# A two-block network in one program: a last weighted sum on TensorE, skipped expert blocks with other waits, keys rounded by two engines, one early load

## The chip, the cores and the metric

The kernel runs on one core of one Trainium2 chip. The core has five engines that run in parallel, each with its own list of instructions, and they meet only through semaphores: TensorE (PE in the rows; PEld is its weight load), VectorE (DVE), ScalarE (ACT), GpSimd (POOL), and SyncE (SP), which here does nothing but start DMAs. The metric is the device time of one execution in microseconds. A change is faster, the same or slower by the times of both kernels in turn on one chip.

## The reference

The computation is two transformer-like blocks over 2048 tokens of width 1024, all in 32-bit floats, then a last norm.

```python
def first_block(x, ...):
        h = _rms_norm(x, pre_norm_g[l]);  z = h @ w_in[l]
        z_q, z_kv, z_kr, g_attn, u_ssm, g_ssm = jnp.split(z, split_points, axis=-1)
        attn = _mla_attention(z_q, z_kv, z_kr, positions, ...)      # 4 heads, one shared rotary key
        ssm = _s5_bidirectional(u_ssm, ...)                         # 32 groups of 64 states
        mixed = jnp.concatenate([attn, ssm], axis=-1) @ w_out[l]
        x = x + _rms_norm(mixed, post_norm_g[l])

def second_block(x, c, ctx, ...):
        attn_x = _attend(qa, [ka_c, ka], [va_c, va])                # 8 heads over 2 key heads, 2304 keys
        ret_x = _ret_output(_retention_latent(...), ...)
        x_new = x + gt1 * (jnp.concatenate([attn_x, ret_x], axis=-1) @ w_out[l])
        y = _hier_moe(h2, ...)                                      # 2 of 32 experts for each token
        x_new = x_new + gt2 * y
    return _rmsnorm(x, final_norm_g)
```

In the mixture of experts, each token goes to two experts. Tokens are sorted by expert and padded to blocks of 128, so that one block has one expert: `(silu(x @ w_gate) * (x @ w_up)) @ w_down`. The result of a token is the sum of its two rows, each times its weight. How many blocks are needed depends on the data: at most 63.

## The kernel before

The program is a row of stages. Each is a block of code with one function for each engine, and a stage starts when every engine has left the one before. Tokens are worked in 16 tiles of 128. Between stages the data lies in DRAM (`between_...` tensors). In the order of time: `project_1`, `attention` (first block), `s5`, `mix_1`, `project_2`, `attention_2`, `retention`, `mix_2`, `dispatch`, `experts`, `combine`.

Many products are made exact enough out of TensorE's faster float format (F32R in the code): a matrix is split into a high part, which fits that format, and a low part, the rest; then three products (high by high, high by low, low by high) are added up. Each split costs a rounding and a subtraction on other engines.

**attention** (`attention`, from L730). The keys are split once, before and within the first tile: five sets of 128 by 2048 (one rotary set and four heads). For each set, VectorE masks the low bits (`high_part`, L723), writes the high part (L1066) and subtracts 5/8 of the columns (L1067), and GpSimd subtracts 3/8 (L864). The raw keys are loaded into two buffers `KX`, so set n waits for the split of set n - 2. Head 0 needs two sets, each later head one; VectorE does the set of head h + 1 right behind the scale of head h (`top_of`, L1028). TensorE's scores of a head (L916) wait for both subtractions. In the tiles behind the first, no key is split.

**mix_1** (from L1408). The states `YS` are loaded in two halves of the columns (L1454), the first by SP and ACT. Its tile loop writes x1 to DRAM. In turn 4 SP loads the first bank of the next stage's weights.

**project_2** (from L1749). X of tile 0 is loaded (L1818), squared, scaled, turned by TensorE, modulated and split (L1922 to L1991); then ACT and DVE split five banks of weights in turn (L1972, L2055), each as it arrives, and TensorE starts a bank when its split is done (L1898).

**attention_2** (from L2060). 32 units (16 tiles by 2 key heads) of 18 steps. A step is a score, exp (L2246) and rounding (L2248) on ACT, a subtraction on GpSimd (L2145), and three products. Ahead of a unit, TensorE and VectorE find the maximum of all scores (L2168, L2278). At the start VectorE splits queries and keys, and behind unit 0's maxima the keys of head 1 and both heads of values (L2256, L2258, L2306).

**experts** (from L3073). For each block, SP loads the three weight matrices (2 MB each) if the expert is new, GpSimd gathers 128 rows of tokens by index (L3165) into one of two buffers, ACT and DVE split the weights, and TensorE multiplies. `tiles_in_use` runs a fixed loop over pairs of blocks on each engine; for pairs that no token needs it calls `skipped`, in which each engine only waits for and increments the semaphores that a real block would. TensorE's `skipped` waits for the gathered rows of the next block (L3238), and GpSimd gathers for the skipped blocks too. Behind the loop, one block's hidden values are turned (L3184), multiplied down (L3197), moved (L3270) and stored (L3126).

**combine** (from L3374). For each of 16 tiles, with buffers for 8:

```python
Y1 = w1 * Y1            # ACT, L3434: first gathered row by its weight
Y1 = w2 * Y2 + Y1       # DVE, L3453
Y1 = Y1 * gate          # DVE, L3455
X2 = Y1 + X2            # DVE, L3458
rstd from sum(X2^2)     # ACT, L3427, L3429, then DVE, L3444
Y1 = X2 * rstd * final_g  # DVE, L3446, one tile behind
```

GpSimd gathers Y2 and Y1 of a tile by index (L3416, L3420); SP loads X2, the constants `gate` (L3399) and `final_g` (L3400), and stores the result (L3395). VectorE starts once both constants are there (L3448). The gather of Y1 of tile i + 8 waits until the store of tile i has landed.

## Time and profile before

| what | value |
|---|---|
| median of three runs | 4704.63 us (4699.98 to 4708.75) |
| profiled execution, its own time | 4703.52 us |
| its span, first to last instruction | 4701.7 us |
| TensorE busy | 4155.1 us (88%), mean granted clock 0.944 |
| VectorE busy | 3094.2 us (66%) |
| ScalarE busy | 2335.9 us (50%) |
| GpSimd busy | 1238.6 us (26%) |
| moved by DMA | 701.06 MB |

Busy shares are means over eleven stages with different limits, so they don't say what one stage is worth. The rows further down are read stage by stage: where an instruction starts, what its engine waited for, and how long the group takes. In a row of a timeline, the bracket at the end is the idle time of the engine just ahead of the instruction and what ended it. Granted clock 1.00 is 2.4 GHz of TensorE, 0.50 is 1.2 GHz.

### The profile page before, as it was taken

How to read it: one execution, taken by the hardware profiler on the slowest of the kernel's cores; microseconds unless marked ns; L12 is line 12 of the kernel's file. 1: busy time of each engine (PE TensorE's matmuls, PEld its weight loads, DVE VectorE, ACT ScalarE, POOL GpSimd, SP SyncE). 2: the span in 40 equal slices, each digit the busy share in tenths (PEclk: the TensorE clock that was granted, in tenths of full speed). 3: DMA queues.
4: the chain of work that ended last, by engine and by line, in shares of the span. 5: the costliest groups of instructions: out<-in, count | busy, mean ns of one | idle time of the engine just before them, and what ended most of it. 6: DMA issues, size and time to landing. Idle time of an engine off the chain costs nothing. (4 is left out here: it accounts for less than half of the span.)

```text
span 4701.7 us, 62499 instructions
## 1 busy us (share of the span) xinstructions
PE 4155.1 (88%) x21994; PEld 3447.7 (73%) x21994; DVE 3094.2 (66%) x3968; ACT 2335.9 (50%) x3681; POOL 1238.6 (26%) x805
## 2 busy tenths in 40 slices
PE   7999879999886997999799999997698699999960
PEld 5777668998765886888678788785476588888850
DVE  6676555555476775444477776766655799999866
ACT  3434323333311554323288888883322477777743
POOL 0000032222110000000189999990000022222222
PEclk9999989999998998999899999998899799999985
DMA  5344331111277333222330000008533488888957
GB/s 181 132 150 136 132 116 56 55 55 55 90 219 207 130 100 125 70 67 72 97 138 14 21 14 14 17 9 280 193 129 117 192 335 317 342 328 342 399 217 299
DMA packets 357224, 701.06 MB, mean 149 GB/s; under 512 B 62928, under 2 KB 244304, under 8 KB 339152
## 3 DMA queue, kind: packets, MB, share of 16 engines
q1 hardware_dynamic: 327984, 618.04, 37.8%
q0 software_dynamic: 13824, 50.34, 2.8%
q10 hardware_dynamic: 15264, 30.81, 2.0%
q8 instruction: 78, 1.28, 0.1%
q14 instruction: 74, 0.61, 0.0%
HBM read 585.06 MB, written 194.51 MB: 166 GB/s over the span
## 5 line engine op out<-in xcount | busy, mean ns | idle before, releaser
L2145 POOL TENSOR_TENSOR a_PL<-a_PT,a_PH 128x512 fp32r<-128x512 f32 x576 | 764.9, 1350 | 81.0 <-ACT a_PH L2248 79.9
L3165 POOL DMA_INDIRECT e_XG<-between_h,all_slots x64 | 214.1, 3346 | 1179.9 <-PE e_pT L3173 642.8
L2278 DVE TENSOR_REDUCE a_part<-a_pA 128x1 f32<-128x1024 f32 (+1 forms) x384 | 366.9, 958 | 238.3 <-PE a_pA L2168 235.2
L2246 ACT ACTIVATE a_PT<-a_pB 128x512 f32<-128x512 f32 x576 | 341.1, 592 | 104.3 <-PE a_pB L2191 102.9
L2248 ACT ACTIVATE a_PH<-a_PT 128x512 fp32r<-128x512 f32 x576 | 364.2, 632 | 18.4
L1021 DVE TENSOR_REDUCE a_maxima<-a_pS 128x1 f32<-128x512 f32 x256 | 176.8, 691 | 169.1 <-PE a_pS L916 168.2
L857 POOL TENSOR_TENSOR a_QL<-a_RQ,a_QT 128x512 fp32r<-128x512 f32 x16 | 20.6, 1290 | 987.7 <-DVE a_QP L1056 958.2
L994 ACT ACTIVATE a_PT<-a_pT 128x512 f32<-128x512 f32 x128 | 69.5, 594 | 415.8 <-PE a_pT L934 415.8
L948 PE MATMUL a_pO<-a_V,a_PT 128*128 128x128 f32 x2048 | 249.4, 275 | 0.3 <-DVE a_PT L1034 0.3
L948 PEld LDWEIGHTS a_pO<-a_V,a_PT 128*128 128x128 f32 x2048 | 243.4, 192 | 5.9 <-DVE a_PT L1034 0.6
L2168 PE MATMUL a_pA<-a_KH,a_QA 128*128 128x512 f32 (+1 forms) x640 | 201.3, 382 | 44.3 <-DVE a_KH L2256 17.7
L2203 PE MATMUL a_pO<-a_PH,a_VH 128*128 128x512 f32 x576 | 228.0, 396 | 0.0
L2190 PE MATMUL a_pB<-a_QA,a_KH 128*128 128x512 f32 x576 | 226.1, 392 | 0.7 <-ACT a_QA L2234 0.7
L2206 PE MATMUL a_pO<-a_PL,a_VH 128*128 128x512 f32 x576 | 225.2, 391 | 1.1 <-POOL a_PL L2145 1.1
L2191 PE MATMUL a_pB<-a_QA,a_KL 128*128 128x512 f32 x576 | 225.6, 392 | 0.0
L2204 PE MATMUL a_pO<-a_PH,a_VL 128*128 128x512 f32 x576 | 225.5, 391 | 0.0
L2134 POOL MEMSET a_QA<- 64x1024 f32 x2 | 1.8, 944 | 846.4 <-POOLq L1751 846.4
L3324 DVE TENSOR_TENSOR e_gate_low<-w_gate,e_gate_high 128x4096 fp32r<-128x4096 f32 x48 | 212.2, 4420 | 10.0 <-ACT e_gate_high L3256 9.7
L3256 ACT ACTIVATE e_gate_high<-w_gate 128x4096 fp32r<-128x4096 f32 x48 | 174.4, 3632 | 82.5 <-SPq L3129 45.6
L3256 ACT ACTIVATE e_up_high<-w_up 128x4096 fp32r<-128x4096 f32 x47 | 170.8, 3635 | 86.2 <-DMA w_up<-in_moe_w_up 78.5
L3324 DVE TENSOR_TENSOR e_up_low<-w_up,e_up_high 128x4096 fp32r<-128x4096 f32 x47 | 207.5, 4415 | 2.3 <-ACT e_up_high L3256 2.3
L3324 DVE TENSOR_TENSOR e_down_low<-w_down,e_down_high 128x4096 fp32r<-128x4096 f32 x47 | 207.6, 4417 | 0.0
(552 smaller groups left out, 10707.7 us busy)
## 6 DMA issues: line engine op xcount, KB each, us to landing
w_gate<-in_moe_w_gate SPq DMA_DIRECT2D x49, 2048.0 KB, 7.6
w_up<-in_moe_w_up SPq DMA_DIRECT2D x48, 2048.0 KB, 11.8
w_down<-in_moe_w_down SPq DMA_DIRECT2D x47, 2048.0 KB
between_yb<-e_Y SPq DMA_DIRECT2D x47, 512.0 KB, 7.3
between_x<-m_X SPq DMA_DIRECT2D x32, 512.0 KB, 3.0
r_W<-in_w_ada SPq DMA_DIRECT2D x8, 2048.0 KB, 21.0
between_yb<-a_zeros SPq DMA_DIRECT2D x31, 512.0 KB, 12.9
between_tv<-p_OV SPq DMA_DIRECT2D x16, 576.0 KB, 2.8
```

The source lines that it names most:

```text
L948: mm = pe.matmul(pO[:, 0:dv], PT[:, jj, :], values(V, h, jj), start=jj == 0, stop=jj == key_tiles - 1)
L2145: pool.tensor_tensor(PL[:, t % RING, :], PT[:, t % RING, :], PH[:, t % RING, :].bitcast(F32), ALU.subtract).then_inc(S["p_low"], 1)
L2190: pe.matmul(pB[t % 2][:], KH[g][:, tile], QA1[i % 2][:, heads, :], start=True, stop=False)
L2191: pe.matmul(pB[t % 2][:], KL[g][:, tile], QA2[i % 2][:, heads, :], start=False, stop=True).then_inc(S["s_ps"], 1)
L2203: pe.matmul(pO[u % 2][:], VH[:, j, g, :], high, start=first, stop=False)
L2204: pe.matmul(pO[u % 2][:], VL[:, j, g, :], high, start=False, stop=False)
L2206: pe.matmul(pO[u % 2][:], VH[:, j, g, :], low, start=False, stop=last).then_inc(S["o_ps"], 1)
L2246: act.activation(PT[:, t % RING, :], pB[t % 2][:], ACT.Exp, scale=scale).then_inc(S["p_ready"], 1)
L2248: act.activation(PH[:, t % RING, :], PT[:, t % RING, :], ACT.Copy).then_inc(S["p_high"], 1)
L2278: dve.tensor_reduce(part[:, h, r % (NG2 // G4):r % (NG2 // G4) + 1], src, AX_X, ALU.max).then_inc(S["maxed"], 1)
L3256: act.activation(WH[n][:], raw(n, t)[:], ACT.Copy).then_inc(w_high[n], 1)
L3324: dve.tensor_tensor(WL[n][:], raw(n, t)[:], WH[n][:].bitcast(F32), ALU.subtract).then_inc(w_low[n], 1)
```

## The change

It has seven parts.

1. **attention**: keys are loaded straight into `KL`, all five sets without a wait. The high part is made by one instruction (the write in F32R rounds): by VectorE for set 0, by ACT for the others. The subtraction works in place. GpSimd takes 3/8 of every set but set 1, which VectorE does whole.
2. **mix_1**: the first part of the states is a quarter of the columns, the second three quarters.
3. **x_first**: SP loads tile 0 of x1 in turn 6 of `mix_1` into a buffer that `project_2` uses as its first.
4. **project_2**: the first bank of weights is split ahead of the modulation (ACT) and of the low part (DVE) of tile 0.
5. **attention_2**: ACT rounds the keys and one part of the first queries, GpSimd subtracts for the keys, and the values of head 1 are split one unit later.
6. **experts**: in `skipped` each engine waits only for its own earlier work; GpSimd waits itself for its gather before last. Behind its loop, SP loads all of x2 (four DMAs of 2 MB) into the buffers of the weights. ACT issues the last store.
7. **combine**: ACT makes two diagonal matrices of the weights of each tile, and TensorE adds up the two gathered tiles with four matmuls of 128 by 512 in plain F32 in PSUM; VectorE reads that sum with the gate. The x2 tiles are read where they were loaded.

```diff
 # attention
-                    if n >= 2:
-                        sp.wait_ge(S["k_split"], n - 1)
-                        sp.wait_ge(S["k_split_dve"], n - 1)
                     for rows, src in key_sets[n]:
-                        sp.dma_start(KX[n % 2][rows, :], src).then_inc(k_loaded[n], 16)
+                        sp.dma_start(KL[n][rows, :].bitcast(F32), src).then_inc(k_loaded[n], 16)
...
+        def lower(eng, n, keys):
+            raw = KL[n][:, keys].bitcast(F32)
+            return eng.tensor_tensor(KL[n][:, keys], raw, KH[n][:, keys].bitcast(F32), ALU.subtract)
...
+                    if n != 1:
+                        high_known(pool, n)
+                        lower(pool, n, pool_keys).then_inc(S["k_split"], 1)
...
                     exps(t, h, h % 2)
-
+                    if t.first and h + 3 < len(key_sets):
+                        high_keys(h + 3)
+            def high_keys(n):
+                act.wait_ge(k_loaded[n], 16 * len(key_sets[n]))
+                act.activation(KH[n][:], KL[n][:].bitcast(F32), ACT.Copy).then_inc(S["k_high_act"], 1)
+            high_keys(1)
+            high_keys(2)
...
+                    if n == 0:
+                        dve.wait_ge(k_loaded[0], 16 * len(key_sets[0]))
+                        dve.tensor_copy(KH[0][:], KL[0][:].bitcast(F32)).then_inc(S["k_high"], 1)
+                    high_known(dve, n)
+                    lower(dve, n, slice(0, nk) if n == 1 else dve_keys).then_inc(S["k_split_dve"], 1)
 # mix_1
-            cols = slice(half * NCH // 2, (half + 1) * NCH // 2)
+            cols = (slice(0, NCH // 4), slice(NCH // 4, NCH))[half]
...
+                if i == 6:
+                    sp.wait_ge(stored[0], 32)
+                    sp.dma_start(M["x_first"][:], D["x1"][0:P, :]).then_inc(M["x_first_loaded"], 16)
 # project_2, ACT (the same order on DVE with weights_low and low)
+            square_sum(tile_at(0))
+            for n in range(EARLY):
+                weights_high(n)
+            modulate(tile_at(0))
+            for n in range(EARLY, len(BANKS2)):
+                weights_high(n)
 # attention_2
+            for g in range(HKV):
+                pool.wait_ge(S["k_high"], g + 1)
+                pool.tensor_tensor(KL[g][HD:P, :], KX[g][HD:P, :], KH[g][HD:P, :].bitcast(F32), ALU.subtract).then_inc(S["k_split"], 1)
...
+            act.wait_ge(q_loaded[0], 32)
+            act.activation(QA2[0][HD:P], RQ[0][HD:P], ACT.Copy).then_inc(S["q_high_act"], 1)
+            for g in range(HKV):
+                act.wait_ge(k_loaded[g], 32)
+                act.activation(KH[g][:], KX[g][:], ACT.Copy).then_inc(S["k_high"], 1)
...
+            high_values(0)
             row(0)
+            high_values(1)
...
             split_queries(0)
-            split_keys(0)
             for r in range(NG2):
                 maximum(0, r)
             top_of(0)
-            split_keys(1)
-            for g in range(HKV):
-                dve.wait_ge(S["v_high"], g + 1)
-                dve.tensor_tensor(VL[:, :, g, :], ...)
+            low_values(0)
...
+                if u == 0:
+                    low_values(1)
 # experts: SP behind its loop
+            sp.wait_ge(w_low["gate"], NB + 1)
+            sp.wait_ge(w_low["up"], NB)
+            sp.wait_ge(w_low["down"], NB)
+            rows = D["x2"].rearrange("(n p) d -> p n d", p=P)
+            for n, space in enumerate(M["X2"]):
+                sp.dma_start(space[:].rearrange("p (n d) -> p n d", d=DM), rows[:, 4 * n:4 * n + 4, :]).then_inc(M["x2_loaded"][n], 16)
...
                 if i >= 2:
                     pool.wait_ge(S["t_ps"], i - 1)
+                    pool.wait_ge(x_loaded[i % 2], 16 * (i // 2))
...
+            for b in range(2):
+                pool.wait_ge(x_loaded[b], 16 * (NB // 2 + 1))
 # experts: TensorE's skipped (ACT, DVE and SP in the same way)
-                pe.wait_ge(S["xt_low"], i + 1)
-                pe.wait_ge(w_low["gate"], i + 1)
-                pe.wait_ge(S["silu_ready"], i)
-                pe.wait_ge(S["hh_ready"], i)
+                pe.wait_ge(S["u_ps"], i)
+                pe.wait_ge(S["d_ps"], i)
+                pe.wait_ge(S["t_ps"], i + 1)
+                pe.wait_ge(S["g_ps"], i)
                 pe.sem_inc(S["ht_ps"], 1)
                 pe.sem_inc(S["g_ps"], 1)
-                pe.wait_ge(x_loaded[nxt.b], 16 * nxt.n + 16)
                 pe.sem_inc(S["t_ps"], 1)
...
+            pe.wait_ge(S["ht_high"], NB - 1)
+            pe.wait_ge(S["ht_low"], NB - 1)
             hidden_transposed(tile_at(NB - 1))
 # combine
+            for i in range(NT):
+                for n in range(2):
+                    d = act.activation(diagonal[n][:, i, :], C["ident"][:], ACT.Copy, scale=M["weights"][:, n, i:i + 1])
+                d.then_inc(S["diagonal_ready"], 1)
...
+                pe.wait_ge(y1_loaded[b], 16 * (i // DEEP + 1))
+                for h in range(2):
+                    cols = slice(h * BANK, (h + 1) * BANK)
+                    pe.matmul(pS[i % len(pS)][:, h, :], diagonal[0][:, i, :], Y1[b][:, cols], start=True, stop=False)
+                pe.wait_ge(y2_loaded[b], 16 * (i // DEEP + 1))
+                for h in range(2):
+                    cols = slice(h * BANK, (h + 1) * BANK)
+                    mm = pe.matmul(pS[i % len(pS)][:, h, :], diagonal[1][:, i, :], Y2[b][:, cols], start=False, stop=True)
+                mm.then_inc(S["sum_ready"], 1)
...
-                dve.scalar_tensor_tensor(Y1[b][:], Y2[b][:], M["weights"][:, 1, i:i + 1], Y1[b][:], ALU.mult, ALU.add).then_inc(S["sum_ready"], 1)
                 dve.wait_ge(S["sum_ready"], i + 1)
-                dve.tensor_tensor(Y1[b][:], Y1[b][:], gate[:], ALU.mult).then_inc(S["gated"], 1)
+                dve.tensor_tensor(Y1[b][:], pS[i % len(pS)][:].rearrange("p a b -> p (a b)"), gate[:], ALU.mult).then_inc(S["gated"], 1)
```

## Rows read from the trace of the kernel before

**Rows 1.** Chain that ended last, last stage: start us, us, what
```profile
4675.99 1.29 DVE c_Y L3453
...
4691.74 1.28 DVE c_Y L3446
```
**Rows 2.** Timeline from the last experts to the last stage: start us, us, engine, line
```profile
4577.43 0.94 POOL L3165 DMA_INDIRECT e_XG<-between_h,all_slots  x1 [1.48 <-PEq L3238]
4583.25 1.11 PE L3184 MATMUL e_pH<-all_ident,e_HH 128*128 128x128 f32 x4 [42.82 <-DVEq L3366]
4594.50 0.36 SPq L3126 DMA_DIRECT2D between_yb<-e_Y  x1
4598.17 0.94 POOL L3416 DMA_INDIRECT c_Y<-between_yb,all_dest  x1 [19.80 <-PEq L3376]
4609.75 1.28 DVE L3453 SCALAR_TENSOR_TENSOR c_Y<-c_Y,all_weights 128x1024 f32<-128x1024 f32 x1 [24.04 <-ACT c_Y L3434]
```
**Rows 3.** Busy time in a stretch: PE, PEld, DVE, ACT, POOL, PEclk, DMA share, GB/s
```profile
4624.00:4676.00 52.00, 0.00 (x0) 0.00 (x0) 50.96 (x52) 26.87 (x43) 16.14 (x15) 0.50 1.03 419
```
**Rows 4.** DMA of 4604 to 4620: queue, packets, MB, share; then the last stage's issue
```profile
q0 software_dynamic: 912, 3.34, 51.3%
...
c_final_g<-in_final_g SPq DMA_DIRECT2D x1, 512.0 KB, 8.6
```
**Rows 5.** DMA issues of 4540 to 4598: queue, times, median us to landing
```profile
e_XG<-between_h,all_slots POOLq DMA_INDIRECT x14, 5.0
```
**Rows 6.** VectorE's last semaphore line in skipped blocks: ns min/median/max, first and last start
```profile
L3366 DVEq EVENT_SEMAPHORE  x16: 21/21/21, 4545.9 to 4583.1; - x16
```
**Rows 7.** Timeline of the retention stage: 32 matmuls in plain F32
```profile
3215.44 14.00 PE L2622 MATMUL r_pR<-r_W,r_alone 128*128 128x512 f32 x32 [0.88 <-DMA r_W<-in_w_ada]
```
**Rows 8.** Waits of 578 to 700, the start of the first attention
```profile
PE a_pS L916 <- POOL a_KL L864: 36.5, 4, 23.6
```
**Rows 9.** Timeline of the same start: first key mask, first scores, scales of heads 0, 3, 4
```profile
589.10 1.23 DVE L723 TENSOR_SCALAR a_KT<-a_KX 128x2048 int32<-128x2048 int32 x1 [3.01 <-DMA a_KX<-between_kr]
...
600.38 0.76 PE L916 MATMUL a_pS<-a_KH,a_QP 128*128 128x512 f32 x1 [23.61 <-POOL a_KL L864]
...
607.66 0.15 DVE L1028 TENSOR_SCALAR a_bias<-a_top 128x1 f32<-128x1 f32 x1
...
653.75 0.15 DVE L1028 TENSOR_SCALAR a_bias<-a_top 128x1 f32<-128x1 f32 x1
...
663.70 0.15 DVE L1028 TENSOR_SCALAR a_bias<-a_top 128x1 f32<-128x1 f32 x1
```
**Rows 10.** Its key instructions: ns min/median/max, first and last start
```profile
L1067 DVE TENSOR_TENSOR a_KL<-a_KX,a_KT x5: 1481/1484/1484, 591.5 to 641.3; 128x1280 fp32r<-128x1280 f32 x5
...
L864 POOL TENSOR_TENSOR a_KL<-a_KX,a_KT x5: 2910/2982/2983, 591.7 to 641.5; 128x768 fp32r<-128x768 f32 x5
```
**Rows 11.** Timeline of the start of the second projection
```profile
1818.66 1.06 ACT L1922 ACTIVATE p_HF<-p_X 128x1024 f32<-128x1024 f32 x1 [9.40 <-DMA p_X<-between_x]
...
1826.23 3.60 ACT L1972 ACTIVATE p_WH<-p2w_w_in 128x4096 fp32r<-128x4096 f32 x1
...
1834.43 3.75 PE L1898 MATMUL p_pZ<-p_WH,p_HH 128*128 128x512 f32 x8 [11.29 <-DVE p2w_w_in L2055]
...
1841.67 3.64 ACT L1972 ACTIVATE p_WH<-p_WL 128x4096 fp32r<-128x4096 f32 x1 [1.78 <-DMA p_WL<-between_w_in]
...
1850.55 2.00 PE L1898 MATMUL p_pZ<-p_WH,p_HH 128*128 128x512 f32 x8
```
**Rows 12.** Timeline of the start of the second attention
```profile
2357.30 7.99 POOL L2145 TENSOR_TENSOR a_PL<-a_PT,a_PH 128x512 fp32r<-128x512 f32 x3 [18.90 <-ACT a_PH L2248]
...
2362.87 2.67 DVE L2278 TENSOR_REDUCE a_part<-a_pA 128x1 f32<-128x1024 f32 x3
...
2366.94 1.28 POOL L2145 TENSOR_TENSOR a_PL<-a_PT,a_PH 128x512 fp32r<-128x512 f32 x1 [1.65 <-ACT a_PH L2248]
```
**Rows 13.** Timeline of the start of the mixing stage
```profile
1528.36 4.87 DVE L1603 SCALAR_TENSOR_TENSOR m_WL<-m_WL,m1w_out_g,m_WH 128x1024 fp32r<-128x1024 f32 x4 [0.20 <-ACT m_WH L1668]
```

171 lines of the change are left out of this document (80 added, 91 removed).

## The prediction

> **What bounds the kernel now.** I read the waits of the profiled execution stage by stage, since no stage touched by the change has the limit that the shares of the whole would suggest. In the last stage VectorE is the bound: over 52 us it is busy 50.96 us with 52 instructions, five a tile, while TensorE does nothing at a granted clock of 0.50 [rows 3], and the chain that ended last runs along it [rows 1]. It starts at 4609.75 [rows 2] and ends at 4691.74 + 1.28 = 4693.0, so 83.3 us for 16 tiles, a period of about 5.11. Before that, skipped expert blocks hold TensorE idle for 42.8 us [rows 2], VectorE's end of each skip goes from 4545.9 to 4583.1 [rows 6], and gathers issued meanwhile land 5.0 us later [rows 5], into two buffers; GpSimd issues one when TensorE's skip lets it (`<-PEq L3238` [rows 2]). The attention starts with TensorE waiting 36.5 us in four waits for GpSimd's low keys [rows 8, 9]; the second projection starts with 11.3 us of idle TensorE [rows 11]; the second attention with GpSimd idle 18.9 us [rows 12].
>
> **A, keys of the first attention.** Before: mask 1.23 (first at 589.10), write 1.23, DVE subtraction 1.48, GpSimd 2.98 beside it [rows 9, 10]; two sets in turn, scores at 600.38. After, set 0 costs VectorE one write, 589.1 + 1.2 = 590.3, and its subtraction, 591.8. Set 1 is 1 MB, 2.4 us at 419 GB/s [rows 3] behind set 0, so there at 591.5. ACT rounds it: 4096 columns of such a rounding take 3.60 [rows 11], so 2048 take 1.8, to 593.3; VectorE subtracts the whole set, 1.48 x 8/5 = 2.37, to 595.7. Scores then start 4.7 us earlier. The later heads: from the scale of head 0 (607.66) to that of head 3 (653.75) are 46.1 us; the steady distance is 663.70 - 653.75 = 9.95 [rows 9], three of them 29.9. The excess, 16.2 us, is three times mask, write and GpSimd's 2.98 = 5.4 behind each scale. After, the rounding was done by ACT ahead of the scale, and 1.48 to 3.0 us of subtraction fit into the time in which TensorE still multiplies the last head, so nearly all of it goes. I give 1 us back for a colder clock: **-20**. The bounds: -8.5 if only the three masks (3 x 1.27) and the first wait go; -21 if all goes. ACT's three roundings of 1.8 lie between exps; should they not be hidden, they cost 5.4. What is late next is the score itself.
>
> **B, mixing.** A quarter of the states lands earlier by up to 2.4 us, but what starts VectorE at 1528.36 is ACT's rounding of the output weights [rows 13], whose load doesn't move. **-0.5** (0 to -2.4).
>
> **C, second projection.** With tile 0 there at the start, ACT squares as soon as the stage is entered, at about 1815.3, and not at 1818.66 behind a load [rows 11]; then it rounds bank 0 (3.60) to 1820.5, modulates to 1824.5, VectorE's low part ends at 1825.0, and TensorE starts there and not at 1834.43: -9.4. But banks arrive at the pace of DMA. Bank 3's rounding starts at 1841.67 after a wait for its load [rows 11], and with loads only some 1.3 us earlier (one transfer of 0.5 MB gone from the queue, 1.2 at 419 GB/s, and a little more) ACT is held there again. Bank 3's matmuls, which ran at 1850.55 [rows 11] behind TensorE's late start, no longer queue; the last bank's split, 3.64 and 4.43 apart on two engines behind bank 3's landing at 1840.4, sets the end of tile 0, about 6.3 us earlier: **-6.3**, an estimate between the 5 that one bank's place gives and the -9.4 of no DMA limit. The order of bank 0 and the modulation changes nothing that is counted twice: both are on ACT. The load in mixing turn 6 passes SP's stores there; 0.5 MB at 419 GB/s [rows 3] is 1.2 us in a stage that isn't bound by DMA, 0 (at most 1.2).
>
> **D, second attention.** VectorE's split of keys and values sits between unit 0's and unit 1's maxima, which start at 2362.87; GpSimd's fourth subtraction comes at 2366.94 [rows 12]. Now ACT does the writes (its exps start some 1.1 us later) and GpSimd subtracts keys while it was idle (18.9 us); its fourth subtraction comes at about 2362.7. GpSimd bounds this stage, so a shift at its start stays: **-4** (-1 to -6). The values of head 1 are split later, before unit 1 needs them.
>
> **E, skipped blocks and the load of x2.** Engines no longer wait for gathers: a block's skip took 37.2 / 15 = 2.48 us [rows 6], the pace of a gather's 5.0 in two buffers; with that gone I take half of it, bounded by 0.5 and 2.48. VectorE would be through at about 4566. GpSimd though still gathers for skipped blocks, two buffers, 5.0 landing each [rows 5], and waits itself for the last. It issued its last at 4577.43 [rows 2], landing at 4582.4; at its own pace the last landing is at 4581, and with x2 loads beside it at about 4583. TensorE's last block, 4583.25 to the store's landing at 4597.4 (14.2 us [rows 2]), now begins at about 4567 and ends at 4581. So the last stage starts at 4583.4, not 4597.4: -14. If x2 slows the gathers (5.0 becomes 8) it starts up to 4592; if not at all, 4581.
>
> **F, the last stage.** Each tile loses one of VectorE's five instructions (1.28 [rows 1], 1.32 with the gap). The multiply by the gate now reads PSUM; no row has that exact pair, the span I allow is 1.22 to 1.5, and I take the SBUF price. 83.3 - 16 x 1.32 = 62.2 us; minus some 1 us of stalls, **61.2**, 3.8 a tile. TensorE: four matmuls a tile in plain F32 at 14.00 / 32 = 0.4375 [rows 7], 1.75 at full clock, 3.5 at the half clock that this stage has [rows 3]; below 3.8, hidden. ACT makes 32 diagonals, 0.11 each by columns (3.60 x 128 / 4096) and a fixed part, 0.3 taken, 10 us, before the first norm and while gathers land, and loses its 16 weightings; hidden. GpSimd's gather of a tile now waits for a store as before.
> When does VectorE start? x2 is 8.4 MB, begun at about 4567.6. DMA moves 419 GB/s in all [rows 3], and the gather queue took 51.3% of it where both had work [rows 4]. By 4583.4 about half of x2 has landed; 4.2 MB, then 1 MB of constants, are 5.2 MB at 0.21 MB/us = 24.6 us: the constants, which landed 8.6 us after their issue [rows 4], now land at 4608. VectorE starts at 4608, hardly before 4609.75, and ends at 4669.2. The change of the tail is then 4669.2 - 4693.0 = **-23.8**. It contains E: the 14 us are eaten by the wait for constants. Afterwards DMA has gathers 16.8 MB, stores 8.4, x2 4.2, constants 1: 30.4 MB / 0.42 = 72 us from 4583, to 4656, under VectorE's end. Bounds: -36 with the constants early; +20 below.
> The Trainium skill, "DMA: Bandwidth & Descriptors", section "Queues, rings and completion order", says that a DMA engine takes turns between queues and takes the descriptors of one ring in order. The 51.3% agrees; the order would hold the constants behind x2, whereas without it VectorE could start at about 4596.
>
> **Sum.** -20 - 0.5 - 6.3 - 4 - 23.8 = -54.6. The profiled execution took 4703.5 (span 4701.7), so 4649; the median is 1.1 higher: **4650**.
>
> **The rivals.**
> 1. Constants early. For: they landed in 8.6 us [rows 4] and x2 may be through or share fairly. Against: 9.4 MB in one queue. VectorE starts 12.2 us into the stage as before (4609.75 - 4597.5), at 4595.6, ends 4656.8: tail -36.2, total -67.0, **4638**. Chance 0.23.
> 2. Little comes from the attention: ACT's roundings delay exps (5.4) or GpSimd's 2.98 stays behind the scale; part A is -9: **4661**. For: TensorE waited for exactly GpSimd [rows 8]. Against: the steady distance leaves slack. Chance 0.13.
> 3. TensorE becomes the bound of the last stage, at half clock with four passes through the array for each plain F32 matmul. One f32r matmul of 512 columns took 3.75 / 8 = 0.47 at the start of the second projection, when TensorE had just been idle [rows 11]; four are 1.88, 7.5 a tile against 3.8. 16 x 7.5 = 120 us from about 4595, 5 more for the last tile on VectorE: 4720, tail +27, total **4701**. For: no row has plain F32 at half clock with weights that change. Against: in the retention stage the row gives 0.4375, against 2.00 / 8 = 0.25 [rows 7, 11], 1.75 times and not 4. Chance 0.03.
> The Trainium skill, "FP8 and Floating Point Precision", section "TensorE Precision Notes", gives true FP32 four passes through the array; the 1.75 times does not agree.
> 4. Slower than before: the same, with weight loads not hidden. A load of 128 columns at a quarter of 1.88 is 0.47, so 2.35 a matmul, 9.4 a tile, 150 us: end 4750, tail +57, less 30.8 elsewhere: **4731**. It decides from (4693.0 + 30.8 - 5 - 4595) / 16 = 7.7 us of TensorE a tile; below 3.8 it costs nothing. Speaks for it: every matmul pair of the sum has another diagonal; against: 3.5 by the retention row. Chance 0.04.
> That the change doesn't do what it says is possible at the skips: if the gathers still set the stage's start (4592), the landing of x2 is by volume, not by start, and VectorE's begin moves by 0 to 3; it stays inside the forecast.
>
> **How the numbers follow.** Forecast 0.57, rivals 0.23, 0.13, 0.03, 0.04. The likeliest one gives 4650. The low end takes in rival 1 with part C at its better bound, 4630; the high end takes in rival 2, PSUM at 1.5 (16 x 0.28 = 4.5) and a late start, 4670. Two tenths of a per cent, 9 us, is about what a measurement of this kernel can tell from no change. Faster by more: forecast, rivals 1 and 2, 0.93. Within: 0.03 (rival 3). Slower: 0.04 (rival 4).
>
> **What would show it.** First scores near 595.5, and scales of heads 0 to 3 some 30 us apart: A. TensorE's first L1898 near 1815 + 10 in its own stage: C. Fourth GpSimd subtraction 4 us sooner: D. Period of the last stage 3.8 with VectorE at 98%, and the wait ahead of its first instruction ending with a constant: F. TensorE's four matmuls over 3.8 us a tile, or VectorE waiting for `sum_ready` in each tile, would make it wrong; so would a first instruction under 14 us after the stage's start (rival 1).

## Result and profile after

The changed kernel took 4680.51 us (median of four runs, 4678.99 to 4684.18), the kernel before 4703.82: ratio 0.9949, interval 0.9934 to 0.9964. In a later comparison the same two kernels gave 4676.26 and 4705.10, ratio 0.9922 (0.9904 to 0.9940). The medians are 23.3 and 28.8 us apart, and the two ratios, which are not those of the medians, stand for 24 and 37 us. Both intervals lie below 1, so there is a gain of half a per cent or a little more. It is not the 54 us of the forecast. The profiled execution has a span of 4677.2 us, 24.5 less than before.

The first instruction of each stage in both traces gives this account, one profiled execution of each kernel. The first two rows are taken at VectorE's first instruction on the queries, since the first instructions of the stage differ. What lies behind the last stage is 0.3 us shorter. How far a stage moves between executions of the same code is said where it matters.

| stage | before us | after us | difference | forecast |
|---|---|---|---|---|
| up to the first attention | | | -1.1 | 0 |
| first attention | | | -14.5 | -20 |
| s5 (no edit) | 232.9 | 240.8 | +7.9 | 0 |
| mixing | 312.7 | 314.8 | +2.1 | -0.5 |
| second projection | 508.2 | 504.1 | -4.1 | -6.3 |
| second attention | 869.0 | 862.7 | -6.4 | -4 |
| retention, mix_2, dispatch (no edit) | 500.7 | 501.7 | +1.0 | 0 |
| experts | 904.2 | 912.8 | +8.7 | -14 |
| last stage | 95.9 | 78.3 | -17.6 | -9.8 |

The last two lines together are -9.0 against -23.8: here lies the largest miss. The last stage itself gained more than forecast, and its start came later than in the kernel before, seen from the start of the expert stage. The pair of executions matters here: the kernel before took 904.2 and 908.0 us for the expert stage (e11), and the code of the changed kernel's expert stage took 907.2 to 912.8 in seven executions (besides the one here e6 907.2, e3 907.5, e5 907.6, e1 910.8, e7 911.4, e10 912.0). With e10 and e11 in place of the first pair, both stages together are -12.9 (991.0 against 1003.9), still little more than half of the forecast. The stretch of [rows 2] in the changed kernel (start us, us, engine and line, idle time ahead in brackets):

```profile
4551.99 0.94 POOL L3210 DMA_INDIRECT e_XG<-between_h,all_slots  x1 [2.08 <-DMA e_XG<-between_h,all_slots]
4552.59 1.09 PE L3231 MATMUL e_pH<-all_ident,e_HH 128*128 128x128 f32 x4 [24.86 <-DVEq L3405]
4552.63 0.40 SPq L3198 DMA_DIRECT2D w_gate<-between_x  x1
4563.10 0.42 ACTq L3357 DMA_DIRECT2D between_yb<-e_Y  x1
4577.78 0.94 POOL L3210 DMA_INDIRECT e_XG<-between_h,all_slots  x1 [3.31 <-DMA e_XG<-between_h,all_slots]
4590.94 0.34 SPq L3437 DMA_DIRECT2D c_gate<-between_gates  x1
4599.38 3.61 PE L3482 MATMUL c_pS<-c_Y,c_diagonal 128*128 128x512 f32 x4 [37.43 <-DMA c_Y<-between_yb,all_dest]
4604.81 1.22 DVE L3502 TENSOR_TENSOR c_Y<-c_pS,c_gate 128x1024 f32<-128x1024 f32 x1 [49.78 <-issue]
...
4667.58 1.28 DVE L3496 SCALAR_TENSOR_TENSOR c_Y<-w_down,c_rstd,c_final_g 128x1024 f32<-128x1024 f32 x1
```

TensorE waits 24.9 us in the skipped blocks and no longer 42.8, and the store of the last result is issued at 4563.1. But then nothing computes until 4590.9. GpSimd issues gathers for blocks that no token needs until 4577.8. What ends the stage is in the view of one line, the one with which every engine ends the block of the stage (count, ns min/median/max, first and last start). GpSimd's instructions there and those of SP, which waits for the last store:

```profile
L3112 POOLq EVENT_SEMAPHORE  x2: 17/17/17, 4590.7 to 4590.8; - x2
L3112 POOLq COMPARE_BRANCH  x1: 33/33/33, 4585.3 to 4585.3; - x1
L3112 POOLq DRAIN  x1: 5284/5284/5284, 4585.4 to 4585.4; - x1
L3112 SPq COMPARE_BRANCH  x1: 38/38/38, 4571.1 to 4571.1; - x1
L3112 SPq DRAIN  x1: 7/7/7, 4571.2 to 4571.2; - x1
```

GpSimd's branch comes at 4585.3, when its wait for the last gathers is over, and behind it its DRAIN (the instruction with which an engine ends its part of a block) takes 5.28 us. The other engines enter the last stage behind its semaphore instructions, at 4590.9. SP was through at 4571.2, so the last store had landed by then, and 19.6 us of this very execution lie between the two. In e10 it is 19.4 (4574.1, 4593.5). In the kernel before, a drain of 7.88 us began at 4577.2 and lay beside TensorE's last block, so it cost nothing:

```profile
L3075 POOLq DRAIN  x1: 7883/7883/7883, 4577.2 to 4577.2; - x1
```

In the last stage itself, before, changed kernel, over the whole stage (columns as in [rows 3]):

```profile
4597.51:4693.39 95.88, 0.00 (x0) 0.00 (x0) 80.31 (x80) 42.10 (x65) 32.44 (x32) 0.50 0.88 355
```
```profile
4590.94:4669.22 78.28, 59.19 (x128) 25.23 (x128) 59.88 (x64) 33.84 (x81) 34.83 (x32) 0.87 0.87 328
```

VectorE has 64 instructions and not 80, as forecast. TensorE has 128 records and 59.2 us of work, where the prediction had 64 matmuls and 28 us: each plain F32 matmul stands in the trace as two records. With this work the granted clock of the stage is 0.87 and no longer 0.50.

### The profile page after: what moved, and what is told of

Same layout as the page of the kernel before. It is cut to its first block and busy times, and to the rows that moved or that the text cites. A ratio compares the mean times of both kernels' runs of the same rounds, so it can differ in the third digit from the quotient of the medians.

```text
span 4677.2 us, 62795 instructions
## 1 busy us (share of the span) xinstructions
PE 4219.9 (90%) x22122; PEld 3475.6 (74%) x22122; DVE 3053.4 (65%) x3938; ACT 2340.2 (50%) x3704; POOL 1234.7 (26%) x806
## 5 line engine op out<-in xcount | busy, mean ns | idle before, releaser
L2285 ACT ACTIVATE a_PH<-a_PT 128x512 fp32r<-128x512 f32 x576 | 364.2, 632 | 18.4
L2197 PE MATMUL a_pA<-a_KH,a_QA 128*128 128x512 f32 (+1 forms) x640 | 200.0, 379 | 37.8 <-ACT a_KH L2272 17.6
## 6 DMA issues: line engine op xcount, KB each, us to landing
r_W<-in_w_ada SPq DMA_DIRECT2D x8, 2048.0 KB, 21.1
```

Source lines behind the costliest of these rows:

```text
L2285: act.activation(PH[:, t % RING, :], PT[:, t % RING, :], ACT.Copy).then_inc(S["p_high"], 1)
```

## Experiments

All are built on the changed kernel unless said otherwise; ratios are against the kernel before. Stage times are from one profiled execution each, so a difference of a few us in the expert stage or in s5 isn't shown by one of them. In the diffs, comment lines and `...` stand for code that is not shown.

### e1: the first attention as before

The function `attention` is the one of before, whole.

```diff
-                        sp.dma_start(KL[n][rows, :].bitcast(F32), src).then_inc(k_loaded[n], 16)
+                    if n >= 2:
+                        sp.wait_ge(S["k_split"], n - 1)
+                        sp.wait_ge(S["k_split_dve"], n - 1)
+                        sp.dma_start(KX[n % 2][rows, :], src).then_inc(k_loaded[n], 16)
...
-            high_keys(1)
-            high_keys(2)
...
+                    high_part(dve, KT[:], KX[n % 2][:]).then_inc(S["k_masked"], 1)
```

> The changed kernel with the first attention as it was before. Theory: the attention part of the change is worth 14.7 us in the profile (stage 687.7 to 671.1 us with its start 1 us earlier), so the stage is back at about 689 us. The s5 stage, which no edit touches, took 232.9 us before and 240.8 us after; theory: that is the granted clock, which depends on when the stage is entered, so s5 is back near 233 us and the whole is 4680.5 + 14.7 - 7.9 = 4687 us. Rival: the 7.9 us come from something that stays in this kernel (buffers laid elsewhere, one more early buffer), s5 stays at 241 us and the whole is 4695 us.

Measured: 4684.78 us, ratio 0.9955 (0.9937 to 0.9973). From the stage's entry, SP's semaphore instruction, the attention took 688.6 us, as against 675.0 in the changed kernel, 689.6 in the kernel before and 688.7 in e11. So its part is worth 13.7 to 14.7 us. (The 673.0 of the expectations, and the figures given with e5 and e9, count from the stage's first DMA, 2.0 us behind the entry.) s5 took 233.6, and the total rose little, as the first theory had it. e10 and e11 take this up again: it isn't settled by one execution.

### e2: x2 loaded in the last stage

```diff
 # experts, SP
-            for n, space in enumerate(M["X2"]):
-                sp.dma_start(space..., rows[:, 4 * n:4 * n + 4, :]).then_inc(M["x2_loaded"][n], 16)
 # combine, SP, behind gate and final_g
+            for n, space in enumerate(M["X2"]):
+                sp.dma_start(space..., rows[:, 4 * n:4 * n + 4, :]).then_inc(M["x2_loaded"][n], 16)
```

> The changed kernel, but x2 is loaded by SP in the last stage, behind the two constants, into the same buffers. Theory: the last eight gathers of the expert stage, 4.2 us apart beside the x2 load, go back to the 3.0 us apart that they had before it began; the last lands 5 us earlier and with GpSimd's drain of 5.3 us the last stage starts at about 4586, not 4591. VectorE starts 12 to 14 us later, and DMA has 34.6 MB in it, 82 us at 0.42 MB/us, so it ends at about 4669 as now: total within 5 us of 4680.5. Rival: the gathers' pace is GpSimd's own and not contention, the stage starts at 4591 and the load of x2 comes on top: +5 to +15 us.

Measured: 4679.73 us, ratio 0.9940 (0.9923 to 0.9956), the same as with the early load. The experts took 901.6 us (912.8 with it), the last stage 90.6 (78.3): 992.2 against 991.1. So the early load gives 12 us to the last stage and takes 11 from the one ahead, through the gathers. Against the 907.2 to 912.8 of the same code it takes 6 to 11. Their pace is in the views of the gather's line, before, changed (from x2's load on), and e2:

```profile
L3165 POOL DMA_INDIRECT e_XG<-between_h,all_slots x14: 937/939/4426, 4541.9 to 4577.4; - x14
```
```profile
L3210 POOL DMA_INDIRECT e_XG<-between_h,all_slots x7: 936/937/939, 4552.0 to 4577.8; - x7
```
```profile
L3207 POOL DMA_INDIRECT e_XG<-between_h,all_slots x11: 936/936/938, 4535.9 to 4566.3; - x11
```

From the first to the last start: 35.5 / 13 = 2.7 us a gather before, 25.8 / 6 = 4.3 beside the load, 30.4 / 10 = 3.0 without it. The theory of contention holds: over the 24 us around the last gathers DMA moved 413 GB/s in the changed kernel (4559 to 4583), near the 419 of [rows 3], and 193 in e2 (4545 to 4569). The stage ends after 901.6 us and not 14 us under 904.2 even so: the gathers alone are slower than the prediction had them, and the drain comes on top.

### e3: the tanh ahead of the key roundings

```diff
+            act.wait_ge(S["c_loaded"], 48)
+            act.activation(half_c[:], cc[:], ACT.Tanh, scale=0.5).then_inc(S["tanh_done"], 1)
             high_keys(1)
             high_keys(2)
-            act.wait_ge(S["c_loaded"], 48)
-            act.activation(half_c[:], cc[:], ACT.Tanh, scale=0.5).then_inc(S["tanh_done"], 1)
```

> The changed kernel with ACT's tanh of the conditioning ahead of its two first key roundings. Theory: VectorE's first maximum waited until 600.7 us for that tanh, which stood behind the rounding of set 2 (landing at 596.7), while the first scores were there at about 597; the first scale comes about 3.3 us earlier than 603.39, and the attention stage is 3 us shorter. Rival: TensorE's second head then waits for the keys instead (the wait moves), and the scale of head 1 at 614.2 and all later ones stay where they are: 0 us.

Measured: 4670.66 us (4662.41 to 4680.13), ratio 0.9918 (0.9898 to 0.9938). The stage got 0.9 us shorter and not 3: 674.0 us against 675.0 from its entry. The first maximum came at 596.93 and not at 600.69, and the first scale at 601.99, 18.4 us behind VectorE's first write of queries as against 19.2. TensorE's twenty score products, from 594.4 to 601.0 and at first at half clock, end last there. The wait for the tanh was real and cost 0.8 us, not 3.3; the lead is kept to the scale of head 3, and the rest of the wait moved to the scores. The rival is nearer, with its 0. What the total has less than that of the changed kernel lies in stages without this edit (s5 237.1 us, experts 907.5).

### e4: gathers only for blocks in use

```diff
-            for i in range(NB + 1):
-                ...
-                pool.indirect_dma_start(out=XG[i % 2][:], ...)
-            for b in range(2):
-                pool.wait_ge(x_loaded[b], 16 * (NB // 2 + 1))
+            gather(0)
+            gather(1)
...
+            used = pool.value_load(in_use, min_val=1, max_val=NB)
+            for j in range(NB // 2):
+                with pool.If(2 * j < used):
+                    gather(2 * j + 2)
+                    gather(2 * j + 3)
+            pool.wait_ge(S["t_ps"], NB + 1)
```

> The changed kernel, but GpSimd gathers only for pairs of blocks in use, through a branch for each pair, and waits at its end for TensorE's count. Theory: what started the last stage at 4590.9 us, 27.8 us after TensorE's last work, are the gathers of skipped blocks beside the x2 load (last landing 4585.2) and GpSimd's drain of 5.3 us behind them. Without them the stage starts when the last store has landed, about 4571 to 4574, VectorE starts behind the constants at 4583 to 4590 instead of 4604.8, and the total is 4660 to 4667 us. Rival 1: x2 and constants set VectorE's start by volume: it moves by no more than the volume of eight gathers, 4.2 MB or 10 us. Rival 2: the branches cost GpSimd time in blocks in use, and gathers get late there: no gain or a loss.

Measured: 4650.64 us (4649.65 to 4651.47), ratio 0.9876 (0.9859 to 0.9892). The experts took 892.4 us, 20.4 less than in the changed kernel (14.8 to 20.4 less than the seven executions of its code) and 11.8 less than before; this is near the forecast's 14 for the stage. The last store, issued at 4553.73, landed 7.9 us later, and the last stage began at 4562.07: the store, and no longer GpSimd, sets it. GpSimd's drain, 3.98 us here, began at 4538.7 and was hidden. VectorE started at 4578.64, 16.6 us into the last stage, which took 80.0. What it waited for is the first sum, not the constants:

```profile
4562.74 0.94 POOL L3456 DMA_INDIRECT c_Y<-between_yb,all_dest  x1 [87.74 <-POOLq L3112]
...
4572.41 3.75 PE L3488 MATMUL c_pS<-c_Y,c_diagonal 128*128 128x512 f32 x4 [19.84 <-DMA c_Y<-between_yb,all_dest]
...
4575.95 2.57 PE L3492 MATMUL c_pS<-c_Y,c_diagonal 128*128 128x512 f32 x4
...
4578.64 1.23 DVE L3508 TENSOR_TENSOR c_Y<-c_pS,c_gate 128x1024 f32<-128x1024 f32 x1 [33.87 <-issue]
```

9.7 us go until the first gather has landed, 6.1 into the first tile's products at half clock. VectorE's start moved 17.7 us towards the start of the expert stage, more than the 10 of the volume. Both rivals, volume and branches, fall.

### e5: the last key set on GpSimd alone

```diff
-                        lower(pool, n, pool_keys).then_inc(S["k_split"], 1)
+                        lower(pool, n, slice(0, nk) if n == 4 else pool_keys).then_inc(S["k_split"], 1)
...
-                    pe.wait_ge(S["k_split_dve"], sets_of_head(h))
+                    pe.wait_ge(S["k_split_dve"], min(sets_of_head(h), 4))
...
+                    if n == 4:
+                        continue
                     high_known(dve, n)
```

> The changed kernel, but the last of the five key sets is subtracted by GpSimd alone (2048 columns, 4.9 us at the 1.83 of its 768) and not by VectorE for 5/8. Theory: VectorE's subtraction at 624.24 us took 4.61 us and not 1.48, since it ran into GpSimd's 3.6 us multiplication of the conditioning, which had begun 0.4 us earlier; it ends with it. Head 3 got late by that: its scale stood 13.96 us behind that of head 2, where 9.95 is steady. Without it the distance is 10 to 11 us, and the attention stage is 3 to 4 us shorter. Rival: head 3 is late for the queries or the clock (three matmuls at 0.63 us), and the distance stays 14.

Measured: 4670.13 us (4669.68 to 4677.61), ratio 0.9924 (0.9907 to 0.9940). The first attention took 669.1 us and not 673.0. The total shows less: e10's executions of the changed kernel, 4659 to 4682 us, reach on both sides of it. The changed kernel first (the scale of heads 2 and 3, the subtraction, GpSimd's multiplication), then e5:

```profile
623.88 3.62 POOL L886 TENSOR_TENSOR a_ada_t<-a_ada_w,all_cs 128x2048 f32<-128x2048 f32 x1
...
624.17 0.15 DVE L1041 TENSOR_SCALAR a_bias<-a_top 128x1 f32<-128x1 f32 x1
624.24 4.61 DVE L805 TENSOR_TENSOR a_KL<-a_KL,a_KH 128x1280 fp32r<-128x1280 f32 x1
...
638.13 0.15 DVE L1041 TENSOR_SCALAR a_bias<-a_top 128x1 f32<-128x1 f32 x1
```
```profile
623.59 0.15 DVE L1041 TENSOR_SCALAR a_bias<-a_top 128x1 f32<-128x1 f32 x1
633.55 0.15 DVE L1041 TENSOR_SCALAR a_bias<-a_top 128x1 f32<-128x1 f32 x1
```

13.96 us became 9.96, the steady distance. The instruction that takes 1.48 us elsewhere took 4.61, and ended (628.85) 1.35 us behind GpSimd's (627.50). Where VectorE started first it was GpSimd that was late: beside VectorE's 1.49 us from 589.25, GpSimd's subtraction from 589.37 took 3.05 us, and 1.83 where VectorE ran no such instruction (619.38). The second attention, with no other edit, took 865.9 us here and 862.7 in the changed kernel (again 865.9 in e9, which shares this edit, and 862.6 to 863.5 in all nine others with this stage as in the change); why isn't known, and it gives most of the gain back.

### e6: eight matmuls a tile

```diff
-                for h in range(2):
+                for n, h in enumerate((0, 1, 0, 1, 0, 1)):
                     cols = slice(h * BANK, (h + 1) * BANK)
-                    pe.matmul(pS[i % len(pS)][:, h, :], diagonal[0][:, i, :], Y1[b][:, cols], start=True, stop=False)
+                    pe.matmul(pS[i % len(pS)][:, h, :], diagonal[0][:, i, :], Y1[b][:, cols], start=True, stop=n < 4)
```

> The changed kernel, but in the last stage the two products of the first gathered row are made three times, so eight matmuls of 128 by 512 in plain F32 a tile and not four; the sum is the same. Theory: one such matmul costs 0.86 us of TensorE at full clock (the trace has two records of about 0.43 for each), so a tile takes 3.43 us as it is and 6.9 us here: TensorE is the bound, the last stage takes about 78 + 16 x 3.1 = 125 to 130 us and the whole 4728. Rival (the prediction's price, 0.4375 for one matmul): 3.5 us a tile, under VectorE's 3.8: no change.

Measured: 4720.30 us, ratio 1.0037 (1.0025 to 1.0049); the last stage:

```profile
4582.73:4709.38 126.65, 112.58 (x256) 49.50 (x256) 60.97 (x64) 33.83 (x81) 34.36 (x32) 0.94 0.55 203
```

Within the theory's 125 to 130. The 128 matmuls of the source stand as 256 records, and one matmul of the source costs 112.58 / 128 = 0.88 us. In the change itself TensorE takes 3.5 us a tile, just under VectorE's 3.8; the prediction had 1.75.

### e7: three parts undone

```diff
 # project_2, ACT and DVE
-            for n in range(EARLY):
-                weights_high(n)
             modulate(tile_at(0))
-            for n in range(EARLY, len(BANKS2)):
+            for n in range(len(BANKS2)):
                 weights_high(n)
 # attention_2 as before; combine: the sum as before, x2 where it was loaded
+                act.activation(Y1[b][:], Y1[b][:], ACT.Copy, scale=M["weights"][:, 0, i:i + 1]).then_inc(S["y1_ready"], 1)
+                dve.scalar_tensor_tensor(Y1[b][:], Y2[b][:], M["weights"][:, 1, i:i + 1], Y1[b][:], ALU.mult, ALU.add).then_inc(S["sum_ready"], 1)
```

> The changed kernel with three parts as before, in three stages that do not meet: in the second projection the order of the first bank and the modulation (the early load of x stays), the whole second attention, and the last sum on ScalarE and VectorE (x2 still read where it was loaded). Theory: second attention back to 869 us from 862.7 (+6.3); second projection 504.1 plus at most 1 (the early load carries its gain); last stage five VectorE instructions a tile again, 78.3 + 16 x 1.3 = 99 us (+21). Sum +28: 4708 us. Rivals: the order of the first bank carries the gain of the second projection, which then goes back to 508; the last sum is worth less than its instructions, since the stage starts as late, and VectorE's start comes earlier without the half-clock sums: 93 us.

Measured: 4691.34 us, ratio 0.9964 (0.9952 to 0.9977). The second attention took 869.0 us, the second projection 504.8: the early load of x carries the gain there. What the order of the first bank is worth isn't shown: with it, the stage took 501.8 to 505.5 us in eleven executions. The total came out 17 us under the theory's 4708; the last stage is 7 of it. The last stage:

```profile
4587.67:4679.71 92.04, 0.00 (x0) 0.00 (x0) 80.25 (x80) 41.15 (x65) 34.11 (x32) 0.50 0.75 279
```

92.0 against 78.3: the rival's 93. VectorE started 9.6 us into the stage here, 13.9 with the sums on TensorE, so of the 21.1 us of removed instructions 4.3 go to the first sum, some 3 to later short waits, and 13.7 remain. Of the 17.6 us of the last stage the other 3.8 are left for x2 being there, the one part of the change in this stage that e7 keeps.

### e8: half of x2 in the last stage, on e4

```diff
-            for n, space in enumerate(M["X2"]):
+            for n, space in list(enumerate(M["X2"]))[:2]:
                 sp.dma_start(...)
 # combine, SP, behind the constants
+            for n, space in list(enumerate(M["X2"]))[2:]:
+                sp.dma_start(...)
```

> The kernel that gathers only for blocks in use, and only the first half of x2 is loaded in the expert stage; SP loads the second half in the last stage behind the constants. Theory: the last store and the first gathers share DMA with 4.2 MB less, so the stage starts some 3 us earlier than behind the whole load, the first sum is there after 12 and not 16.6 us, and the whole is 3 to 6 us shorter: 4645 us. Rival: the last stage is then bound by volume (27.5 + 4.2 MB, 75 us at 0.42 MB/us): VectorE waits for gathers, and the time is the same or up to 5 us longer.

Measured: 4653.24 us (4648.54 to 4658.67), ratio 0.9885 (0.9868 to 0.9901), no better than e4. Experts 888.8 us, last stage 81.0, together 969.8 against 972.4 of e4. VectorE still started 17.3 us into the last stage (4585.90 against 4568.60). The start came earlier as expected, the first sum didn't. Differences of 2 or 3 us in one execution each are less than the expert stage moves in the same code, so half or all of x2 early is not told apart here.

### e12: all of x2 in the last stage, on e4

The edit is that of e2 on e4.

```diff
 # combine, SP, behind gate and final_g, and not in experts
+            for n, space in enumerate(M["X2"]):
+                sp.dma_start(...)
```

> Gathers only for blocks in use, and all of x2 loaded in the last stage behind the constants: what the early load is worth once the gathers are out of its way. Theory: the last store lands without company and the stage starts at about 888 to 890 us of the expert stage, not 892.4; VectorE then shares the volume of 34.6 MB, 82 us, and the last stage takes 88 to 91 us and not 80: both together 978, so 6 us more than with the early load. Rival: the early load is worth nothing, since the sum of both stages is bound by VectorE either way: 972 within 2.

Measured: 4659.23 us (4651.70 to 4667.62), ratio 0.9895 (0.9876 to 0.9914). Experts 886.5 us, last stage 90.4, together 976.9 against 972.4: with the gathers out of its way the early load is worth 4.5 us in these executions, with them (e2) 1.1. The theory said 6. The spread of the expert stage, 5.6 us, is as large as these differences.

### e9: three edits together

The edits of e4, e5 and e8.

```diff
+                with pool.If(2 * j < used):
...
+                        lower(pool, n, slice(0, nk) if n == 4 else pool_keys)
...
+            for n, space in list(enumerate(M["X2"]))[:2]:
```

> The changed kernel with three things of the runs before together: gathers only for blocks in use, half of x2 loaded in the last stage, the last key set subtracted by GpSimd. Theory: they lie in different stages and add up: 991.1 to about 969.8 us for experts and last stage, 673.0 to 669.1 for the attention, so 25 us off 4680.5: 4655 in the same clock of the s5 stage, down to 4645 with the best seen there (230.7 us), 0.988 of before. Rival: the parts share a gain and it stays at the 4650.6 of the gathers alone or above.

Measured: 4648.34 us (4638.83 to 4649.11), ratio 0.9866 (0.9849 to 0.9884): the lowest of all, but its interval overlaps that of e4. First attention 669.0 us, experts and last stage 968.6, second attention 865.9, s5 234.8.

### e10 and e11: both kernels once more

No edit in either.

```diff
 # e10: the changed kernel as it is
 # e11: the kernel before as it is
```

> The changed kernel itself once more. Theory: the 7.9 us that s5 lost, a stage with no edit, are the granted clock of that execution: over the profiles so far s5 took 230.7 us with 34.1 us at half clock and 244.7 with 61.4, a half microsecond for each. So s5 here takes another time than 240.8, on the same line (232 at 36 us, 241 at 54). Rival: the loss comes with the program (its buffers or code), and s5 takes 240.8 within 1 us again.

> The kernel before once more, for its stages: does s5 take 232.9 us (47.8 at half clock) again? If the loss of the changed kernel belongs to the program, 233 within 1 us; if it is the clock of an execution, any value from 230 to 245 on the line of half a microsecond for each one at half clock. The other stages, first attention 689.6, second projection 508.2, second attention 869.0, should come back within 1 us.

Measured: e10 4676.26 us (4659.41 to 4682.41), ratio 0.9922 (0.9904 to 0.9940); e11 4708.04 us in one execution. The whole of s5 in both kernels, twice, and in e4 and e8, which share its code and all ahead of it with the changed kernel (TensorE's granted clock is the third number from the end). Before and e11:

```profile
1269.67:1502.61 232.94, 173.30 (x832) 142.03 (x832) 145.78 (x217) 36.01 (x64) 27.84 (x20) 0.90 0.74 214
```
```profile
1266.52:1503.29 236.77, 175.57 (x832) 143.76 (x832) 145.58 (x217) 36.08 (x64) 28.83 (x20) 0.89 0.73 210
```

The changed kernel and e10:

```profile
1254.04:1494.87 240.83, 178.34 (x832) 145.75 (x832) 145.66 (x217) 36.12 (x64) 29.20 (x20) 0.88 0.73 207
```
```profile
1255.67:1496.57 240.90, 177.57 (x832) 145.47 (x832) 143.64 (x217) 36.14 (x64) 28.02 (x20) 0.88 0.72 207
```

e4 and e8:

```profile
1252.57:1483.23 230.66, 169.53 (x832) 139.69 (x832) 145.73 (x217) 35.98 (x64) 27.18 (x20) 0.92 0.75 216
```
```profile
1255.23:1499.91 244.68, 180.50 (x832) 147.32 (x832) 143.65 (x217) 36.21 (x64) 28.76 (x20) 0.87 0.71 203
```

That the time goes with the clock is shown: over the fourteen profiled executions s5 took from 230.7 us, with 35.9 us of it at half clock, to 244.7, with 63.0, and the straight line through all has 0.49 us for each microsecond at half clock. Whether the change makes the clock worse there isn't settled. Against it: the kernel before moved by 3.8 us between two executions, e4 was faster than any, and the other kernels that share all code up to the end of s5 with the changed one took 235.6 (e7), 236.7 (e2), 237.2 (e6) and 237.3 us (e12). For it: the changed kernel gave 240.8 and 240.9, as e10's rival had it, and the eight executions of that code have a mean of 238.0 against 234.9 of the two before. The other stages of e11 came back within 1 us as expected, but for the expert stage, 908.0 us as against 904.2.

## Why the prediction was wrong

**The step that failed is E**: "So the last stage starts at 4583.4, not 4597.4: -14." Moved by the 15.2 us that the changed kernel is ahead at the start of the expert stage, that is 4568.2; it started at 4590.94, 22.8 us late. The first half of the step, engines that skip faster, was right: TensorE's last block began at 4552.59, 30.7 us ahead of before, of which 15.4 are its own (forecast 16). The second half was not: that GpSimd's gathers would be over some 2 us behind the last block, at 4583. Three things stand in its place, from the runs. The load of x2 slowed the last gathers from 3.0 to 4.3 us each and cost 6 to 11 us (e2). The gathers alone ran at 3.0 us and not at the 2.5 assumed. And behind the last landing GpSimd drained for 5.3 us, which nobody else's work hid any more. e4, which takes the gathers away, brought 15 to 20 us back, about the 19.6 between SP's end and GpSimd's, and so shows the cause as a whole. How much belongs to each of the three is less sure, and no run takes the drain away alone. The prediction had named contention as a bound ("If x2 slows the gathers (5.0 becomes 8) it starts up to 4592", 4576.8 in the changed kernel's time), and had set it aside since constants behind x2 were to be late anyway. The start came 14.1 us behind even that bound. The drain it didn't have, though it stood in the trace of before, hidden.

**F, the last stage.** "VectorE starts at 4608" rested on the wrong mechanism. x2 had landed when the stage began (the last of its four loads 33.4 us behind its issue at 4554.18, so at 4587.6), and VectorE waited 13.9 us, not for a constant: its last wait is the one for the first sum, and ended at 4604.74, 0.04 us behind that sum. This was the place of rival 1 (12.2), and its sign, a start under 14 us into the stage, came, if with another wait behind it. Moved by the 15.2 us, VectorE started at 4620.0, 12.0 us behind the forecast: a stage that began 22.8 us late, less the 10.7 us by which the wait in it was shorter than the 24.6 forecast. That it wasn't further off is luck, two errors against each other. Whether constants wait behind x2 in a queue was not put to the test in the changed kernel, since x2 had landed before they were issued.

The other 2.9 us of the 14.9 are VectorE's own stretch: 64.1 us from its first to its last, against 61.2. Price of an instruction and count were right, 1.28 and 16. TensorE's price was half of what it is, since [rows 7], which calls them 32 matmuls, shows 32 records of 16 matmuls: 14.00 / 16 = 0.88 us each, at a granted clock of 1.00. That VectorE still set the pace was close, 3.5 against 3.8 us a tile at full clock. At half clock it would have been 7.2 (the first four records, two matmuls, took 3.61 us) and near rival 3's 7.5. The granted clock was 0.50 over the stage in e7, where TensorE did nothing, and 0.87 with its sums. In e6 a record took 0.44 us on the average. Against the 2.00 / 8 = 0.25 us of an F32R matmul of this size [rows 11], 0.88 is 3.5 times. The Trainium skill, "FP8 and Floating Point Precision", section "TensorE Precision Notes", has four passes for true FP32. By that rule, these runs agree nearly, and the prediction's 1.75 times, its ground for setting the rule aside, was a misreading of the records.

**A, the first attention.** -14.7 by the scale of head 3 (638.13 against 653.75, less the 0.95 by which the stage began earlier), forecast -20. First scores came where they were forecast: 4.5 us earlier against 4.7. Of the missing 5.3 us, 4.0 are VectorE's subtraction behind GpSimd's multiplication (e5). Another 0.9 lie between heads 0 and 1 (10.83 against 9.95). The forecast had counted the order of all engines but not what GpSimd does next beside VectorE. VectorE's 4.61 us beside GpSimd's 3.62, and e5's steady distance without the meeting, are what the rows show. The Trainium skill, "GPSIMD Engine Reference", section "Specifications", says that GpSimd shares its way to SBUF with VectorE and that VectorE's instructions with two SBUF inputs meet it there, as this subtraction has. By that rule, the trace agrees.

**C, the second projection.** TensorE started 9.6 us into the stage, as forecast (9.7), against 19.1 before. Then it waited for banks whose loads had not come earlier: ACT's roundings each end a wait for DMA in the changed kernel,

```profile
1822.41 5.42 ACT L1983 ACTIVATE p_WH<-p_WL 128x4096 fp32r<-128x4096 f32 x2 [3.85 <-DMA p_WL<-between_w_in]
1830.77 3.62 ACT L1983 ACTIVATE p_WH<-p_WL 128x4096 fp32r<-128x4096 f32 x1 [2.93 <-DMA p_WL<-between_w_in]
1836.16 3.63 ACT L1983 ACTIVATE p_WH<-p_WL 128x4096 fp32r<-128x4096 f32 x1 [1.78 <-DMA p_WL<-between_w_in]
```

and 4.1 us are left of the 9.5. The rounding of bank 3 began 26.5 us into the stage, as against 26.3 before, where the forecast had its load 1.3 us earlier. So the forecast had the right limit, and its 6.3 was 2.2 too high.

**D, the second attention.** -6.4 against -4, confirmed by e7 (869.0). The order of the forecast holds; the size was low.

**B, mixing.** The first states came 2.6 us earlier (VectorE's first `m_yt` 7.5 us into the stage, 10.1 before), and it was lost at the output weights as forecast. Then TensorE made the first tile's products at half clock:

```profile
1527.22 3.68 PE L1703 MATMUL m_pM<-m_WH,m_CH 128*128 128x512 f32 x8 [4.20 <-DVE m_CL L1606]
```

3.68 us where the kernel before took 2.14, and the lead of 0.5 us over the kernel before, seen from the start of the stage, turned into 1.0 us behind it. That makes 1.0 of the 2.1 us that the stage lost; where the other 1.1 lie isn't known.

**s5** lost 7.9 us in this execution without an edit, with more time at half clock (56.3 us and not 48.6). No step of the prediction allowed for it, and whether the change has a part in it stays open.

So of the 30.1 us between forecast and result in the profile, 14.9 are the tail, 7.9 s5, 5.5 the first attention, 4.8 mixing and second projection, less 2.4 of the second attention and 0.4 of the rest.

## What to carry to other kernels

When a stall is taken away, list all that the stage's end waits for, the issuing engine's own drain among it, and ask which of it was hidden only by the stall. Work that exists for nobody (gathers for unused blocks) is worth removing before its waits are rearranged: here (e4) that brought 26 to 30 us on top of the changed kernel, about as much as the whole change. Before a price is taken from a grouped row, count the instructions in the source against the records of the row.

## What the hardware showed

- Each plain F32 matmul of 128 by 512 is two records in the trace, 0.88 us together at full clock, against 0.25 for F32R.
- A VectorE subtraction of 1.48 us that started 0.4 us behind a GpSimd multiplication of 3.62 took 4.61: it ended 1.35 us after it.
- GpSimd's drain at the end of the expert stage took 5.28 us behind the last gather's landing in all eight executions that gather to the end (changed, e1, e2, e3, e5, e6, e7, e10), and 3.98 in the four where the last gather lay far back (e4, e8, e9, e12).
- s5 is 0.49 us longer for each microsecond at half clock. That amount differs between executions of one kernel: the kernel before took 232.9 and 236.8 us.
- The same code of the expert stage took 907.2 to 912.8 us in seven executions.
